# Two-layer hybrid trunk: S5 matrix steps in halves, at other blocks, and the phase work moved and doubled

## What is computed

```python
u = rmsnorm(h)                                   # (528, 1024)
q, k, v, a_lr, ..., = split(u @ w_in)            # 10512 columns
# GLA: per chunk of 64, gates by head
log_a = log_sigmoid(a_lr @ w_a2 + b_a) / 16
g = cumsum(log_a within the chunk)
d_state = (k * exp(g_end - g))^T v ;  decay = exp(g_end)
# S5: 64 groups of 16 channels, 64 complex states each
bb = cf * b                                      # complex, from a, dt
x_t = ab * x_{t-1} + bb u_t ;  y = Re(c x) + d_skip * u
y = gelu(y); y = y * sigmoid(y @ w_glu)
h = h + (sum of three gated branches) @ w_out
```

## Time and profile before

| | us |
|---|---|
| Time, median of 3 runs (1890.87 to 1894.38) | 1894.04 |
| Span of the profiled execution, first to last instruction | 1894.7 |
| TensorE busy | 1747.2 |
| VectorE busy | 927.3 |
| GpSimd busy | 788.6 |
| ScalarE busy | 701.2 |

### The profile page before, as it was taken

The page is one execution under the profiler, slowest core; times in us unless marked ns, Lnnn a source line. Parts: engine busy times, 40 slices in busy tenths (PEclk is TensorE's granted clock), DMA queues, the critical chain, the costliest instruction groups (busy, mean ns, idle before and its releaser), DMA issues.

```text
span 1894.7 us, 31165 instructions
## 1 busy us (share of the span) xinstructions
PE 1747.2 (92%) x12985; PEld 1538.7 (81%) x12985; DVE 927.3 (49%) x1471; ACT 701.2 (37%) x1332; POOL 788.6 (42%) x490
## 2 busy tenths in 40 slices
PE   5967899999998999988997999999999898999997
PEld 4967798999887889987897987777788676788885
DVE  7985134333438992374453222533334598624223
ACT  3453442444543113332233543334455322224322
POOL 1655575333232223332343685653332332344442
PEclk8988999999999999998898999999999998999999
DMA  8543244322375653535342433542223956433432
GB/s 146 149 108 105 72 115 118 85 67 72 92 153 131 158 146 107 112 82 149 87 124 55 133 90 90 113 118 78 67 75 101 169 156 155 124 100 92 143 104 85
DMA packets 363539, 209.56 MB, mean 111 GB/s; under 512 B 75524, under 2 KB 350136, under 8 KB 360840
## 3 DMA queue, kind: packets, MB, share of 16 engines
q1 hardware_dynamic: 350600, 187.92, 38.7%
q10 hardware_dynamic: 12800, 19.66, 3.5%
HBM read 170.34 MB, written 36.67 MB: 109 GB/s over the span
## 4 chain that ended last, share of the span: by engine, by line
PE 68%; DVE 10%; POOL 7%; DMA 5%; ACT 5%; issue 3%; SPq 2%; ACTq 1%; DVEq 0%; POOLq 0%
PE ring L844 52%; DMA sb_w_raw<-in_w_in 4%; POOL sb_w_lo L686 3%; PE ring L803 3%; DVE sb_s_prod L1631 2%; PE ring L825 2%; PE aux L1115 1%; SPq L580 1%; PE aux L1224 1%; PE aux L1160 1%; PE aux L1136 1%; DMA s_matrices<-sb_s_phase 1%; DVE sb_s_rot L2136 1%; DVE sb_s_rot L1631 1%; PE aux L1163 1%
## 5 line engine op out<-in xcount | busy, mean ns | idle before, releaser
L686 POOL TENSOR_TENSOR sb_w_lo<-sb_w_raw,sb_w_hi 128x1024 fp32r<-128x1024 f32 x246 | 609.0, 2477 | 1026.3 <-ACT sb_w_hi L1275 1023.9
L1275 ACT ACTIVATE sb_w_hi<-sb_w_raw 128x1024 fp32r<-128x1024 f32 x246 | 260.0, 1057 | 602.7 <-DMA sb_w_raw<-in_w_in 398.7
L844 PE MATMUL ring<-sb_u_hi,sb_w_hi 128*128 128x264 f32 (+1 forms) x2112 | 368.5, 329 | 24.6 <-DVE sb_tmp_dve L1711 14.6
L844 PEld LDWEIGHTS ring<-sb_u_hi,sb_w_hi 128*128 128x128 f32 x2112 | 314.3, 203 | 63.3 <-DVE sb_tmp_dve L1711 16.5
L844 PE MATMUL ring<-sb_u_lo,sb_w_hi 128*128 128x264 f32 (+1 forms) x2112 | 340.8, 312 | 0.0
L844 PE MATMUL ring<-sb_u_hi,sb_w_lo 128*128 128x264 f32 (+1 forms) x2112 | 334.6, 309 | 0.0
L844 PEld LDWEIGHTS ring<-sb_u_lo,sb_w_hi 128*128 128x128 f32 x2112 | 300.6, 192 | 22.0
L844 PEld LDWEIGHTS ring<-sb_u_hi,sb_w_lo 128*128 128x128 f32 x2112 | 294.1, 188 | 21.0
L1307 ACT ACTIVATE sb_tmp_act<-ring 128x528 f32<-128x528 f32 (+1 forms) x112 | 67.3, 601 | 138.6 <-PE ring L844 135.8
L1746 DVE SCALAR_TENSOR_TENSOR sb_tmp_dve<-sb_tmp_act,ring 128x528 f32<-128x528 f32 (+1 forms) x32 | 22.3, 696 | 142.0 <-PE ring L844 130.0
L1551 ACT ACTIVATE sb_att_scores<-sb_att_scores,sb_att_neg_max 128x208 f32<-128x208 f32 x128 | 58.5, 458 | 82.7 <-DVE sb_att_neg_max L1929 82.7
(11 more groups left out here) (333 smaller groups left out, 2455.7 us busy)
## 6 DMA issues: line engine op xcount, KB each, us to landing
sb_w_raw<-in_w_in SPq DMA_DIRECT2D x166, 512.0 KB, 4.1
sb_s_loaded<-s_matrices ACTq DMA_DIRECT2D x16, 1040.0 KB
s_matrices<-sb_s_phase SPq DMA_DIRECT2D x16, 528.0 KB, 3.1
sb_w_raw<-in_w_gla_out SPq DMA_DIRECT2D x16, 512.0 KB, 3.5
sb_w_raw<-in_w_attn_out SPq DMA_DIRECT2D x16, 512.0 KB, 3.5
sb_w_raw<-in_s_w_glu SPq DMA_DIRECT2D x16, 512.0 KB, 3.5
sb_w_raw<-in_w_s_out SPq DMA_DIRECT2D x16, 512.0 KB, 3.5
sb_w_raw<-in_w_out SPq DMA_DIRECT2D x16, 512.0 KB, 3.5
```

Of the source, the lines that this page charges most:

```text
L686: pool.tensor_tensor(WL[:, w], WR[:, w], WH[:, w].bitcast(F32), ALU.subtract).then_inc(lo_ready, 1)
L844: last = pe.matmul(RING[:, 2 * r + hf, 0:c1 - c0], w[:, n % SLOTS, kt, :], moving(b[0], xx[:, kt], c0, c1), start=(term == 0 and kt == 0), ...
L1275: act.activation(WH[:, w], WR[:, w], ACT.Copy).then_inc(hi_ready, 1)
```

## The change

- `step_matrices` becomes `steps_turned` (mbm turned, called by `mat_lead` ahead of the block) and `step_products` (behind the block). On ScalarE the mb0 copies (`first_powers`) go ahead of the block too, and the rest of the turn comes directly behind the block's copy for gk, gv and gq. mbm and the skip diagonal have two buffers.
- The turns of set 0 go from one behind each block gk3 to gq0 to gk2, gv0, gv1, gv3, gv4, gv6, gv7, gq1, gq2; those of set 1 from sg2, ws5 and wout to glu3, glu5 to glu7, mg1 2, 4, 6 and wout 1, 3. The start of VectorE's first set of layer 1 goes from sg2-5 to glu2-4, the loads of its B and C from sg0 to glu0, and its buffers lie where S5's loaded matrices were.
- ScalarE does the exponential of the gate before ahead of the log-sigmoid of this one; the log-sigmoids stand at gk3, gv1, gv4, gv7 in layer 0, and as before in layer 1.
- Phase work of layer 0 begins at gq1 with two steps a block, and the spill of phase j stands at block 19 + j. Layer 1 keeps its places.

```diff
-GATE_AT = ((0, 2, 4, 6), (0, 1, 3, 5))
-MATS_0 = [("gk", 3)] + [("gv", j) for j in range(1, 8)] + [("gq", 0)]
-MATS_1 = [("sg", 2)] + [("ws5", j) for j in (0, 1, 2, 3, 5)] + [("wout", j) for j in (0, 2, 4)]
+LOG_AT = ({("gk", 3): 0, ("gv", 1): 1, ("gv", 4): 2, ("gv", 7): 3},
+          {("gv", 0): 0, ("gv", 1): 1, ("gv", 3): 2, ("gv", 5): 3})
+DECAYS_AT = (("gq", 1), ("gv", 7))
+MATS_0 = [("gk", 2)] + [("gv", j) for j in (0, 1, 3, 4, 6, 7)] + [("gq", 1), ("gq", 2)]
+MATS_1 = [("glu", j) for j in (3, 5, 6, 7)] + [("mg1", j) for j in (2, 4, 6)] + [("wout", j) for j in (1, 3)]
+FIRST_SET_AT = [("glu", j) for j in (2, 3, 4)]
...
-PHASE_FIRST = BLOCKS.index(("gv", 0))
+PHASE_FIRST = (BLOCKS.index(("gq", 1)), BLOCKS.index(("gv", 0)))
+PHASE_STEPS = (2, 1)
 PHASE_BASE = 9
-PHASE_SPILL = {BLOCKS[PHASE_FIRST + PHASE_BASE + 2 * j]: j for j in range(KT)}
+PHASE_SPILL = {(ly, BLOCKS[PHASE_FIRST[ly] + (PHASE_BASE + 2 * j + 1) // PHASE_STEPS[ly]]): j
+               for ly in range(2) for j in range(KT)}
...
-            mbm = sb(f"s5_mb{m}", [P, 2, QUADS, 4, S5_GROUP], at=at_bb)
+            mbm = sb(f"s5_mb{m}", [P, 2, 2, QUADS, 4, S5_GROUP], at=at_bb)
...
-              mat_buffers(1, [base, base + WIDE], [o_att, end])]
+              mat_buffers(1, [o_att + 16512, end], [o_att, o_att + 16512])]
...
-                    if name == ("sg", 0) and ly == 0:
+                    if name == ("glu", 0) and ly == 0:
                         ...
                         load_c(1, 0)
                         load_c(1, 1)
...
-                    if b >= PHASE_FIRST:
-                        next(work, None)
+                    if b >= PHASE_FIRST[ly]:
+                        for _ in range(PHASE_STEPS[ly]):
+                            next(work, None)
...
+            def mat_lead(ly, b):
+                if ly == 0 and b in MATS_AFTER and MATS_AFTER[b][1]:
+                    m, k = MATS_AFTER[b]
+                    steps_turned(m, k - 1)
...
                 for b in BLOCKS[2:17]:
+                    mat_lead(ly, b)
                     project(ly, b, UH, UL)
                     mat_turn(ly, b)
...
-            def matrices_out(m, j):
+            def first_powers(m, j):
                 act.wait_ge(mats_ready, 8 * m + j + 1)
+                if j:
+                    aux_result(act, m, ("toep", j - 1))
                 ...
                 last.then_inc(first_power, 1)
+            def matrices_out(m, j):
...
+                    mat_lead(ly, b)
                     block_turn(b)
+                    if kind in ("gk", "gv", "gq"):
+                        mat_turn(ly, b)
...
-                    if kind == "gv" and j in GATE_AT[ly]:
-                        hd = GATE_AT[ly].index(j)
-                        log_sigmoid(hd)
+                    if b in LOG_AT[ly]:
+                        hd = LOG_AT[ly][b]
                         if hd:
                             decay_to_end(hd - 1)
-                    if b == (("gv", 7) if ly else ("gq", 0)):
+                        log_sigmoid(hd)
+                    if b == DECAYS_AT[ly]:
...
-                if j:
-                    aux_result(dve, m, ("toep", j - 1))
+                if j >= 2:
+                    aux_result(dve, m, ("toep", j - 2))
...
-                    if ly == 0 and b == ("sg", 2):
+                    if ly == 0 and b == FIRST_SET_AT[0]:
                         first_set = itertools.chain(input_matrix(1), s5_matrices(1, 0))
-                    if ly == 0 and kind == "sg" and 2 <= j <= 5:
-                        next(first_set)
+                    if ly == 0 and b in FIRST_SET_AT:
+                        for _ in range(2 if b == FIRST_SET_AT[2] else 1):
+                            next(first_set)
```

More of the change, by code:

```diff
@@ L895, in transpose_c, with steps_turned @@
                 last.then_inc(aux_full[h], 1)
-            def step_matrices(m, j):
+            def steps_turned(m, j):
                 pe.wait_ge(mats_ready, 8 * m + j + 1)
@@ L906, in step_matrices, with step_products @@
                             last = pe.matmul(AX_[outs, 2 * h + q % 2, c0:c0 + 64],
[L907 to L908 removed]
+                                             MB[m]["mbm"][ins, j % 2, ri, q].rearrange("p a b -> p (a b)"),
+                                             ID[ins, ins], start=True, stop=True)
                 last.then_inc(aux_full[h], 1)
+            def step_products(m, j):
                 h = aux_take(m, ("toep", j))
@@ L917, in step_matrices @@
                                   start=(ri == 0), stop=False)
-                last = pe.matmul(AX_[:, 2 * h, 0:S5_GROUP], ID[:], MB[m]["dsk"][:], start=False, stop=True)
+                last = pe.matmul(AX_[:, 2 * h, 0:S5_GROUP], ID[:], MB[m]["dsk"][:, j % 2], start=False, stop=True)
                 if j + 2 < KT:
@@ L1239, in _ @@
                 for j in range(1, KT):
+                    mat_lead(ly, ("glu", j))
                     project(ly, ("glu", j), GH, GL)
+                    mat_turn(ly, ("glu", j))
                 for j in range(KT):
                     project(ly, ("sg", j), UH, UL)
-                    mat_turn(ly, ("sg", j))
                 for j in range(KT):
+                    mat_lead(ly, ("mg1", j))
                     project(ly, ("mg1", j), UH, UL)
+                    mat_turn(ly, ("mg1", j))
                     if j == 0:
@@ L1249, in _ @@
                         project(ly, ("ws5", j), YH, YL)
-                    mat_turn(ly, ("ws5", j))
                 project_as_made(ly, ("wout", 0), MXH, MXL, mlo_ready, KT * ly)
-                mat_turn(ly, ("wout", 0))
                 for j in range(1, KT):
+                    mat_lead(ly, ("wout", j))
                     project(ly, ("wout", j), MXH, MXL)
@@ L1345, in matrices_out @@
                         last = act.activation(MB[m]["mb0"][rows, :, x::2, c0:c0 + S5_GROUP],
-                                              MB[m]["mbm"][rows, :, x::2, 0], ACT.Copy)
+                                              MB[m]["mbm"][rows, j % 2, :, x::2, 0], ACT.Copy)
                 last.then_inc(first_power, 1)
+            def matrices_out(m, j):
                 if j:
@@ L1373, in c_turned, with mat_lead @@
                 last.then_inc(aux_free[h], 1)
+            def mat_lead(ly, b):
+                if ly == 0 and b in MATS_AFTER and MATS_AFTER[b][1]:
+                    m, k = MATS_AFTER[b]
+                    first_powers(m, k - 1)
             def mat_turn(ly, b):
@@ L1487, in _ @@
                                        ACT.Exp, scale=1.0 / GLA_TAU).then_inc(dec_ready, 1)
-                    if b == ("sg", 0) and ly == 0:
+                    if b == ("glu", 0) and ly == 0:
                         aux_read(act, 0, ("y", 7))
@@ L1500, in _ @@
                         wout_squares(j - 1)
-                    mat_turn(ly, b)
+                    if kind in ("glu", "mg1", "wout"):
+                        mat_turn(ly, b)
                     if b == ("gq", 3):
```

15 lines of the change are left out of this document (7 added, 8 removed).

## The result

The changed kernel takes 1921.68 us (median of 4 runs, 1917.03 to 1921.75) beside 1894.21 for the kernel before on the same chip: ratio 1.0123 [1.0089, 1.0158]. The forecast was 1906, with 1917 as the upper end. So the sign was right and the size was not: 27 us slower instead of 12.

A forecast was written before the change was run, and what follows sets the result against it. TensorE, busy for 92% of the span, was taken as the bound, other engines mattering only where it waits. 1894.7 - 6.2 + 32.0 - 6.1 - 8.4 gave 1906 us, slower by 0.6%; range 1897 to 1916 (chance 0.62).

The forecast's parts named there:

- the two-step rounds: gg2 to aq1: one phase buffer's round of 12.8 us spans one block, TensorE waiting some 5 us a block.
- (a): Rival: gate loop closes near TensorE's pace, the gate stage gives 24 us instead of 6, whole 1888; chance 0.15.
- (b): Rival: phase rounds are hidden because GpSimd runs ahead and the spill comes early, whole 1880; chance 0.05.
- (c): Rival: phase-round loss holds but gate stage and tail reach halfway to their good ends, 1894 to 1896; chance 0.10.
- (d): Rival: GLU part worse, B and C late and hits in each set, +4 us or more there, 1918; chance 0.08.
- term 4: GLU blocks to wout7, second set's turns moved: 265.4 us instead of 273.8, -8.4; bounds -14 to +4.
- Term 1: Gate stage to the end of gq3: 189.4 us instead of 195.6, -6.2; bounds -24 to +2.
- Term 2: Phase rounds in gg and aq, from the end of gg1 to aq3's start: +32.0 us; bounds +20 to +36.
- Term 3: Three blocks behind the phase rounds, all spills done: 19.3 us instead of 25.4, -6.1; bounds -6 to -3.
- The loop: Gate stage, three blocks each time: serial log-sigmoid, decay, odd set, block; 27.4 us against 20.4 for TensorE's own work.
- The GLU part: glu5 to glu7: sets wanted ahead of the very next blocks, 7.1 us waits and slow blocks, 29.1 us new.

The follow-up runs named there:

- phases alone: The kernel before with only the change's phase work of layer 0 (from gq1, two steps a block, spill j at block 19 + j): 1917.52 us, ratio 1.011.
- control: The changed kernel run once more, unchanged, on another chip: 1913.37 us beside 1891.56 for the kernel before, ratio 1.0104.
- split spill: The changed kernel with each phase spilled in two DMAs, one for each half of the buffer: 1890.55 us, ratio 0.9988.
- spaced tail: The changed kernel with the second set's turns further apart, at glu3, glu6, sg1, mg1 0, 2, 4, 6, wout 1, 4: 1891.65 us, ratio 0.9991.
- whole turns: The changed kernel with steps turned, first powers and products together behind the block: 1874.68 us; the same with layer 0's phases again from gv0: 1864.08 us.

## Why the prediction was wrong

**What bounds the kernel, and the signs.** Right. Each wait that was named appeared at its place: gv0 (6.6 us), gv4 and gv7 (4.8 and 4.9), gq2 (7.3, where 4 to 5 had been said), glu5 to glu7, and six in the low parts of gg and aq. The step on which the sign hung, the two-step rounds, gives the whole loss alone (phases alone, 1.011). Rivals (a), (b) and (c) didn't come. The time lies near the 1918 of (d), but term 4 is not at +4 or more, so (d) didn't come either.

**Sizes.** The forecast sum was +11.3 on the spans; the two profiles of the changed kernel give +25.2 and +16.0.

| step | forecast | changed | control |
|---|---|---|---|
| Term 1, to gg2 | -6.2 | -0.4 | -1.4 |
| Term 2, to block 27 | +32.0 | +35.2 | +34.8 |
| Term 3, to block 33 | -6.1 | -6.3 | -6.2 |
| attention and S5 of layer 0 | 0 | -4.6 | -2.0 |
| Term 4, glu0 to layer 1 | -8.4 | -4.7 | -6.0 |
| layer 1 | 0 | +5.9 | -3.3 |

Terms 1, 2 and 4 were too low by 12.7 and 10.0 together. Each lay inside its bounds, always on the bad side: these sizes are the step that failed, term 1 most. In the first profile layer 1 added 5.9 that the control doesn't repeat.

**Term 1 was mis-sized the most, by 5 to 6 us.** It was worked out to the end of gq3, as -6.2; measured there are -4.2 and -3.6. The way from there to gg2 was put at no change, without a reason, and took 3.8 and 2.2 us more than before. The loop itself was right: from gv4 to gv7 it took 27.34 us (120.44 to 147.78) against 27.4. The next took 29.57, because set 7 lay beside the first phase steps. VectorE in order of time, and the low part on GpSimd under its last row:

```profile
139.30 3.85 DVE L1665 TENSOR_TENSOR sb_s_mat_prod<-sb_s_c,sb_s_powers 128x320 f32<-128x320 f32 x4
...
145.58 0.76 DVE L1665 TENSOR_TENSOR sb_s_mb<-sb_s_mat_prod 128x256 f32<-128x256 f32 x2
...
166.64 2.73 DVE L1665 TENSOR_TENSOR sb_s_mat_prod<-sb_s_c,sb_s_powers 128x320 f32<-128x320 f32 x4
...
172.92 1.03 DVE L1665 TENSOR_TENSOR sb_s_mb<-sb_s_mat_prod 128x256 f32<-128x256 f32 x2
173.75 2.40 POOL L691 TENSOR_TENSOR sb_w_lo<-sb_w_raw,sb_w_hi 128x1024 fp32r<-128x1024 f32 x1
173.99 2.19 DVE L2139 TENSOR_SCALAR sb_s_skip_diag<-sb_eye_by_group,sb_params 128x16 f32<-128x16 f32 x1
```

Set 5 takes 7.3 us, which is the 7.4 of the forecast; set 7 takes 9.5, with nearly all of its groups stretched and the last, 0.23 us elsewhere, standing still for 2.0 until the low part ends. The forecast had kept 7.4 and 1 more for the phases; 2.1 more than 7.4 were measured. By the rule cited there from the Trainium skill, "SBUF — State Buffer", section "SBUF: two separate sides", the exclusive lock would have cost some 3.5 on top of what was kept; the measured loss lies between the two, nearer to what was kept. That it is spread over many groups fits a lock taken by many short instructions, but no run here separates it from other contention.
Two more pieces were not in the sum at all. gq3 ends at 191.35, 4.2 earlier than before, but a group of transposes then waits 1.4 us for ScalarE's copy of k, 0.3 before; turn 8 now lies just ahead of gq3, which may be why, and was not tried. Then the same wait of 2.9 us as in the kernel before is followed by matmuls at the lower level of the clock. First the kernel before, then the changed one:

```profile
218.98 2.00 PE L1022 MATMUL aux<-sb_gla_v_tok,sb_gla_k_tok 64*128 64x256 f32 x16 [2.92 <-ACT sb_gla_o_tok_meta L1454]
```

```profile
215.88 3.79 PE L1038 MATMUL aux<-sb_gla_v_tok,sb_gla_k_tok 64*128 64x256 f32 x16 [2.93 <-ACT sb_gla_o_tok_meta L1484]
219.59 3.13 PE L849 MATMUL ring<-sb_u_hi,sb_w_hi 128*128 128x264 f32 x16
```

So 2.7 more were gone by gg2 (1.4 in the control).

**Term 2 was short by 3.** Five rounds were as worked out: TensorE's fifth wait ends at 302.74, 76.2 us behind the end of gg1, against 11.0 and five times 12.8, 75.0. The sixth took 16.0 and not 14.8: GpSimd stood idle for its buffer for 6.5 us instead of 3.2, behind SP's queue, and the 16 matmuls behind the wait of 8.4 took 3.89 us.

```profile
294.45 1.02 SPq L578 DMA_DIRECT2D sb_bias_meta_meta<-bias_skew  x1
...
302.72 6.25 SPq L585 DMA_DIRECT2D sb_bias_meta<-bias_skew  x4
309.01 0.74 SPq L557 DMA_DIRECT2D s_matrices<-sb_s_phase  x1
```
```profile
318.76 3.89 PE L849 MATMUL ring<-sb_u_hi,sb_w_lo 128*128 128x264 f32 x16 [8.40 <-POOL sb_w_lo L691]
```

The bias loads hold the spill for 14.6 us where the round gives 12.8; the forecast counted 2 of it and none of what follows. The cause, one buffer with its spill between two halves, is shown by the split spill.

**Term 3** held within 0.2.

**Term 4 was short by 2.4 to 3.7.** The GLU part was right: glu4 to sg0 30.5 more, against 29.1 and 1.2. The waits were 6.9, 5.7 and 5.7, with sets at their clear 5.1, so what rival (d) feared, late B and C and a hit in each set, wasn't there. What was missed stands at wout3: its set comes 3.1 us late, not 0.9, which is 2.2 of it. The rest is open.

```profile
998.06 0.69 PE L911 MATMUL aux<-sb_identity,sb_s_mb 64*64 64x64 f32 x32 [3.05 <-DVEq L2140]
```

**Layer 1** was forecast at 0, at most 2 either way. It was +5.9 and -3.3 in two profiles of one kernel. The bound was wrong: it spoke of what the change does and not of how far one execution of this layer differs from the next. The waits that vary are those for VectorE's state in the S5 part: 9.0 us in the first profile, 4.7 in the control. The 0.2% named as the limit of what can be told was too small for the same reason: the kernel before itself ran from 1880.05 to 1903.64 on one chip.

**What the prediction should have tried.** Every part was costed, but no part was costed with its neighbour's lead changed. That steps_turned ahead of a block moves the demand forward was seen; that this alone is worth some 39 us in the whole, with everything else kept, was not: the forecast credited the halves with removing mb0's waits and put the new waits down to the places.

## What to carry to other kernels

Splitting a step so that its first half stands a block earlier also asks for its input a block earlier; where the producer has no lead, the new wait is larger than the one removed, and the same places with the whole step behind the block win. Where the places leave the producer a block of room, as in the spaced tail, the lead pays instead. A buffer that is filled, spilled and filled again put the transfer's whole 3.2 us into each round here; two transfers, one for each half, took it off the chain without any more memory (12.67 to 9.65 us a round). And when the steps per block are doubled, compare the round of the buffer with the new block, not with the old two.

## What the runs showed of the hardware

- Behind the same wait of 2.9 us, 16 matmuls took 2.00 us in the kernel before, 3.79 in the changed one and 3.39 in the control. From gg0 to gg1 the granted clock was 0.87, 0.73 and 0.77. So equal waits don't cost equal amounts, and a sum that prices only waits misses some us; what tips it was not settled.
- VectorE's sets lengthen beside GpSimd's short phase instructions as well as beside its long low parts: in the gate stage with whole turns, 85.7 us of busy time beside 69.6 of GpSimd, 79.8 beside 43.5.
- Two profiles of one kernel stay within 2.5 us of each other over the first 1044 us and differ by 9 in layer 1, partly in waits for VectorE's state (9.0 and 4.7 us in its S5 part).
